# A two-layer hybrid encoder on one core: the groups of the Mamba-2 mixer without modulation tiles, a buffer of its own for the fourth decay piece, and three steps moved between engines

## The chip, the cores and the metric

One NeuronCore of a Trainium2 chip runs the whole program. The metric is the device time of one execution in microseconds; the kernel before took 2819.65 us (median of three).

## The reference, cut to what matters

```python
# SEQ 256, D 2048, two layers, everything float32
cond = silu(c)
shift, scale, gate = split(cond @ ada_w[i, s] + ada_b[i, s], 3)      # i layer, s sublayer: 4 x 6144 columns
h = rms_norm(x, norm_g[i, s]) * (1 + scale) + shift
# layer 0: short convolution mixer, then MLP; layer 1: Mamba-2 mixer, then MLP; x = x + gate * out each time
mlp = square(relu(h @ w1)) @ w2                                       # 2048 -> 8192 -> 2048
# the mixer: 64 heads of 64 in 8 groups, state 128, two chunks of 128 tokens, both directions
z, xbc, dt_raw = split(h @ w_in); xs, B, C = split(silu(conv3(xbc)))
dt = softplus(dt_raw + dt_bias); cum = cumsum(dt * a_neg)             # per direction
y = sum over directions of (C B^T * decay(cum)) @ (dt * xs), plus d_skip * xs
u = group_rms_norm(y * silu(z)) * norm_g; out = u @ w_out
```

## The kernel before, in words

**Units.** Every large product is cut into units: 128 output rows from 2048 input rows and 256 tokens. A unit's weights are two halves of 512 KB, streamed by SP into four `raw` buffers. ScalarE rounds a half into `wh` (`hi`, L687), VectorE makes the rest `wl = raw - wh` (`lo`, L1133), and TensorE runs 32 matmuls, 16 of 512 columns (`wh` against both parts of the input) and 16 of 256 (`wl` against the high part) (`unit`, L936 and L939). Then ScalarE copies the 256 first columns out of PSUM (`copy`, L692) and VectorE adds the others. `lo` of unit v + 2 stands in VectorE's program around the sum of unit v, its first half ahead of the sum and its second behind it. There are 433 units: 48 and 16 of the convolution mixer, 128 of the first MLP, 1 for dt, 50 of groups 0 to 4, 16 of the first half of the mixer's output product, 30 of groups 5 to 7, 16 of the second half, 128 of the second MLP.

**Modulation tiles.** `cond @ ada_w` isn't done on TensorE: 192 tiles of 1 MB are loaded into two buffers `adat`, and VectorE multiplies and sums each (`tile`, L1146), one at the end of some units. Pool keeps the result (`keep`, L496). A tile is only needed when its sublayer begins. The last 48 are shift, scale and gate of the second MLP.

**A group and its scan.** A group is ten units, called slots 0 to 9 here: B, C, four of x, four of z. While group g's units run, the scan of group g - 1 is threaded through them, one piece ahead of each slot on each engine. `scan_piece` stands ahead of a slot's unit and `scan_late` behind it. On TensorE: slot 0 scores and transposes of x; slots 2 to 5 the head products of two heads each, 24 short matmuls (L1049), called batches 1 to 4 here; slot 6 eight transposes; slot 9 two short matmuls that sum squares. On VectorE: `segments` (L1382) makes the exponents of a piece, ScalarE's `decays` (L800) exponentiates them, `masked` (L1313, L1315, L1319) makes the matrix of two heads. Batch k needs piece k, and batch 1 also `xd`, x times dt for both directions, which Pool multiplies (L587) from ScalarE's copies of the transposes (L814). In slot 6 VectorE adds the skip term (L1340) and Pool multiplies by z (L592). In slot 9 ScalarE takes the root (L824), VectorE the reciprocal (L1345) and the scaled result (L1349, semaphore `gu`), ScalarE its high part (L834), Pool its low part (L604, semaphore `u_lo`), which the output product waits for. Pieces 1 and 4 share one buffer, `normt`; so the load of piece 4 waits in slot 2 for batch 1.

**Order.** Every engine runs a program written out by hand, in one order (`walk`); no planner moves anything. SP issues all loads in order, and each load waits until its buffer is free. Groups 1 to 4 are a hardware loop of two iterations of two groups. Group 7's scan runs inside the second half of the output product (`late_outs`), 32 slabs of half a unit, with its slots at the slabs of `SLOT_AT`.

In group 0 the dt path runs in the place of the scan: `dt_late(s)` behind unit s on VectorE, and ahead of it on TensorE. TensorE's part in slot 4 waits for the eleventh of VectorE's small steps.

## Time and profile before

| | us |
|---|---|
| median of 3 runs (2816.4 to 2820.9) | 2819.65 |
| the profiled execution | 2821.6 |
| its span | 2819.9 |

The profiled execution lies 1.7 us above its span and 2.0 us above the median. Times in the rows are us from the start of the span. The page gives, for each engine, the busy time; in 40 slices, its share in tenths and the TensorE clock that was granted; and the chain of work that ended last. The timeline gives each instruction with the idle time before it and what ended that. Stretches can be asked for their busy times and their mean clock.

### The profile page before, as it was taken

What the parts mean: (1) busy time and instruction counts of PE and PEld (TensorE: products, weight loads), DVE (VectorE), ACT (ScalarE), POOL (GpSimd) and SP (SyncE); (2) the same over time, 40 slices, a digit from 0 to 9 for tenths busy, and PEclk for the clock granted to TensorE, in tenths of its full rate; (3) what the DMA queues carried; (4) which work ended last, traced back from release to release, by engine and by line L of the source; (5) the groups of instructions that cost most, each with busy time, mean ns of one, the idle gap of its engine ahead of it and who ended that gap; (6) DMA issues with size and microseconds to landing.
All of it is one profiled execution on the core that took longest, in us unless ns stands there. A gap on an engine that the chain in (4) does not pass through costs nothing.

```text
span 2819.9 us, 46272 instructions
## 1 busy us (share of the span) xinstructions
PE 2607.5 (92%) x14940; PEld 2279.0 (81%) x14940; DVE 2163.9 (77%) x2509; ACT 1359.0 (48%) x2038; POOL 1007.8 (36%) x890
## 2 busy tenths in 40 slices
PE   0399999999999999989999999998999999999998
PEld 0288888888888888878888888887878888888887
DVE  6988889986777779977888878888885555555554
ACT  2244444544444444464555545555455444444454
POOL 3522225442333334534554533555531111111123
PEclk9899999999999999999999999999999999999999
DMA  8888889786877779956565576656646555555554
GB/s 330 308 324 317 304 341 352 242 325 217 285 287 277 281 287 333 356 174 206 202 207 199 180 264 223 208 196 208 228 132 200 187 188 191 187 187 190 189 186 142
DMA packets 171668, 679.60 MB, mean 241 GB/s; under 512 B 18672, under 2 KB 35312, under 8 KB 146704
## 3 DMA queue, kind: packets, MB, share of 16 engines
q1 hardware_dynamic: 171488, 677.75, 68.5%
q8 instruction: 78, 1.28, 0.2%
q14 instruction: 54, 0.44, 0.0%
q0 software_dynamic: 48, 0.13, 0.0%
HBM read 675.58 MB, written 2.23 MB: 240 GB/s over the span
## 4 chain that ended last, share of the span: by engine, by line
PE 73%; DVE 11%; issue 5%; POOL 3%; ACT 3%; DMA 1%; DVEq 0%; ACTq 0%; POOLq 0%; SPq 0%
PE psm L936 45%; PE psm L939 22%; DVE wl L1133 3%; PE psy L1049 3%; DVE adat L1146 2%; ACT wh L687 1%; POOL xd L587 1%; DVE normt L1435 1%; PE psm L1094 1%; PE psr L1094 1%; DMA raw<-in_w 1%; POOL x L534 1%; DVE rbc L1345 0%; PE psm L1097 0%; ACT normt L800 0%
## 5 line engine op out<-in xcount | busy, mean ns | idle before, releaser
L1133 DVE TENSOR_TENSOR wl<-raw,wh 128x1024 fp32r<-128x1024 f32 x862 | 1174.6, 1363 | 410.8 <-ACT wh L687 408.4
L936 PE MATMUL psm<-hcat,wh 128*128 128x512 f32 x3984 | 1269.2, 400 | 5.5 <-DVE tt L1163 4.8
L687 ACT ACTIVATE wh<-raw 128x1024 fp32r<-128x1024 f32 x866 | 911.0, 1052 | 207.6 <-PE psm L939 148.0
L939 PEld LDWEIGHTS psm<-hcat,wl 128*128 128x128 f32 x3984 | 755.8, 190 | 179.7
L936 PE MATMUL psm<-hid,wh 128*128 128x512 f32 x2560 | 806.8, 396 | 11.1 <-POOL hid L604 5.4
L939 PE MATMUL psm<-hcat,wl 128*128 128x256 f32 x3984 | 788.9, 280 | 0.0
L936 PEld LDWEIGHTS psm<-hcat,wh 128*128 128x128 f32 x3984 | 614.4, 191 | 7.2 <-DVE wl L1133 5.5
L939 PEld LDWEIGHTS psm<-hid,wl 128*128 128x128 f32 x2560 | 482.2, 188 | 113.9
L939 PE MATMUL psm<-hid,wl 128*128 128x256 f32 x2560 | 504.1, 278 | 0.0
L1146 DVE CUSTOM_DVE_ANT_0 adat<-adat,cond 128x2048 f32<-128x2048 f32 x176 | 430.3, 2445 | 21.2 <-DMA adat<-in_ada 13.8
L936 PEld LDWEIGHTS psm<-hid,wh 128*128 128x128 f32 x2560 | 391.3, 189 | 12.1 <-POOL hid L604 5.6
L534 POOL TENSOR_TENSOR x<-x,tt 128x256 f32 (+1 forms) x154 | 203.2, 1320 | 404.8 <-DVE tt L1210 404.8
L544 POOL TENSOR_TENSOR hid<-tt,hid 128x256 f32 x128 | 145.6, 1138 | 530.7 <-ACT hid L755 530.7
L496 POOL COPY modc<-modt 128x1 f32 (+1 forms) x192 | 156.4, 820 | 214.8 <-DVE modt L1146 214.7
L692 ACT ACTIVATE ta<-psm 128x256 f32<-128x256 f32 x257 | 97.3, 379 | 209.1 <-PE psm L939 203.8
L692 ACT ACTIVATE ta<-psm,mods 128x256 f32<-128x256 f32 x160 | 75.6, 473 | 223.5 <-PE psm L939 222.6
L755 ACT ACTIVATE hid<-tt 128x256 f32 x128 | 53.5, 418 | 243.2 <-DVE tt L1232 243.2
L1210 DVE SCALAR_TENSOR_TENSOR tt<-psm,mods,ta 128x256 f32<-128x256 f32 x160 | 76.7, 479 | 114.3 <-ACT ta L692 114.1
L572 POOL TENSOR_TENSOR th<-th,acc 128x256 f32<-128x256 f32 x48 | 60.2, 1255 | 242.5 <-ACT th L788 242.5
L958 PE MATMUL psm<-hcat,wh 128*128 128x512 f32 x128 | 47.3, 453 | 77.6 <-POOL wl L669 55.5
L1049 PE MATMUL psy<-xd,normt 128*128 128x64 f32 x384 | 62.0, 335 | 43.4 <-POOL xd L587 37.6
L696 ACT ACTIVATE normt<-x 128x256 f32<-128x256 f32 (+1 forms) x80 | 33.3, 418 | 142.5 <-POOL x L534 100.1
(164 smaller groups left out, 1873.8 us busy)
## 6 DMA issues: line engine op xcount, KB each, us to landing
raw<-in_w SPq DMA_DIRECT2D x866, 512.0 KB, 4.0
adat<-in_ada SPq DMA_DIRECT2D x176, 1024.0 KB, 5.3
xs<-in_ada SPq DMA_DIRECT2D x8, 1024.0 KB, 7.0
zs<-in_ada SPq DMA_DIRECT2D x8, 1024.0 KB, 6.6
normt<-running_sums SPq DMA_DIRECT2D x32, 256.0 KB, 4.6
dec<-running_sums SPq DMA_DIRECT2D x32, 256.0 KB, 5.6
x<-in_xT SPq DMA_DIRECT2D x1, 2048.0 KB, 17.0
out<-x SPq DMA_DIRECT2D x4, 512.0 KB, 2.9
```

The lines of the kernel that those rows point to most:

```text
L496: pool.tensor_copy(modc[:, bass.ds(a.v, 1)], modt[:, a % 2:a % 2 + 1]).then_inc(mod_copied, 1)
L534: pool.tensor_tensor(x[:, nn.v, :], x[:, nn.v, :], tt[:, v % 2, :], ALU.add).then_inc(stored, 1)
L544: pool.tensor_tensor(hid[:, jj.v, T:2 * T], tt[:, v % 2, :], hid[:, jj.v, 0:T].bitcast(F32), ALU.subtract).then_inc(stored, 1)
L572: pool.tensor_tensor(t, t, src, ALU.mult).then_inc(silu_mul, 1)
L687: act.activation(wh[:, h % 4, :], raw[:, h % 4, :], ACT.Copy).then_inc(hi_done, 1)
L692: act.activation(ta[:, v % 2, :], psm[v % 2][:, 0:T], ACT.Copy, scale=scale).then_inc(copied, 1)
L936: pe.matmul(bank[:, :], wh[:, h % 4, (k + i) * P:(k + i + 1) * P], src[:, kb + i, :], start=(kb + i == 0), stop=(kb + i == KB - 1), skip_g ...
L939: mm = pe.matmul(bank[:, T:2 * T], wl[:, h % 4, (k + i) * P:(k + i + 1) * P], src[:, kb + i, 0:T], start=False, stop=(kb + i == KB - 1), s ...
L1049: mm = pe.matmul(psy[ch][:, cols], m[:, at:at + P], xd[:, d, sc, cols], start=(i == 0), stop=(i == 2), skip_group_check=True)
L1133: dve.tensor_tensor(wl[:, h % 4, :], raw[:, h % 4, :], wh[:, h % 4, :].bitcast(F32), ALU.subtract).then_inc(lo_done, 1)
L1146: dve.tensor_tensor_reduce(t, t, cond[:, :], 1.0, 0.0, ALU.mult, ALU.add, modt[:, a % 2:a % 2 + 1]).then_inc(ada_done, 1)
L1210: return dve.scalar_tensor_tensor(out=tt[:, v % 2, :], in0=psm[v % 2][:, T:2 * T], scalar=gcol, in1=ta[:, v % 2, :], op0=ALU.mult, op1=ALU ...
```

## The change

- **Piece 4 has a buffer**: `em[4]` is a part of `adat[:, 1]`. SP loads it right behind piece 3 in slot 0, not in slot 2 behind batch 1.
- **No tiles in groups** (24 before: three in each, slots 4, 5, 8). They go to: the up products of quarters 1 and 2 of the first MLP (three of four units, not two; 8 tiles more), the first output product (12 tiles, not 8), the first 16 units of the second MLP (one in every unit; 16 more). `late_outs` has 4 (slabs 15, 18, 25, 28), not 8 (slabs 1, 4, ..., 22).
- **x copied first**: in slot 0 ScalarE copies the transposes of x (L814) ahead of `decays(g, 1)`, not behind.
- **VectorE multiplies by z** in slot 6, not Pool.
- **Slot 9**: VectorE's reciprocal and its four results (L1345, L1349) stand behind the first `lo` of that slot (`scan_mid`), not ahead of it.
- **Group 0**: `dt_late(1)` and `dt_late(2)` stand ahead of their units on VectorE; the steps of slots 6 and 8 move to 7 and 9.
- **Groups 1 to 4 are written out**, no loop. The first two units of the first output product run interleaved (`pair`), block by block. Head products stay where they are.

```diff
-LATE_TILES = {1 + 3 * k: k for k in range(8)}
+LATE_TILES = {15: 0, 18: 1, 25: 2, 28: 3}
-        em.append(em[1])
+        em.append(adat[:, 1, 0:6 * T].rearrange("p (k t) -> p k t", k=4))
...
-                quarter0(q1, q1 * 16 + (a - 16), (0, 2), False)
+                quarter0(q1, q1 * 20 + (a - 20), (0, 1, 2), False)
...
-                return first_unit(g), (4, 5, 8), g * 3 + a
+                return first_unit(g), (), None
+            for k in range(GA):
+                group(At(k), *g_unit(At(k)))
...
-            bodies(4, lambda i, f: gated(i * 4 + U_OUT0, 2, i * 4, (0, 2), i * 2 + ao, f, False, "chunk 0"))
+                gated(At(U_OUT0 + 4 * k), 2, At(4 * k), (1, 2, 3), At(a + 3 * k), k == 0, False, "chunk 0")
...
-            bodies(4, lambda i, f: relu(i * 4 + U_MLP1, i * 4, i * 4 + 64, 3, (), None, f))
+            bodies(3, lambda i, f: relu(i * 4 + U_MLP1, i * 4, i * 4 + 64, 3, range(4), i * 4 + a, f))
+            relu(At(U_MLP1 + 12), At(12), At(12 + 64), 3, range(4), At(a + 12), False)
...
             def scan_loads(g, s):
-                for piece in {0: (3,), 2: (4,)}.get(s, ()):
-                    load_sums(g, piece)
+                if s == 0:
+                    load_sums(g, 3)
+                    load_sums(g, 4)
...
-                if s == 6:
-                    pool.tensor_tensor(flat(xs, 0, XB), flat(xs, 0, XB), flat(zs, 0, XB), ALU.mult)\
...
-                    decays(g, 1)
                     at_least(act, sg_xt, g + 1)
                     for ch in range(2):
                         act.activation(xd[:, 0, ch, :], psy[ch][:, :], ACT.Copy).then_inc(xt_copied, 1)
+                    decays(g, 1)
...
+                both = first and src == "chunk 0"
+                if both:
+                    pair(u, ready, hid)
...
                 lo(v * 2 + 4)
+                if midway:
+                    midway()
                 at_least(dve, copied, v + 1)
...
+                    dve.tensor_tensor(xs[:, par2, :, :], xs[:, par2, :, :], zs[:, par2, :, :], ALU.mult)\
+                        .then_inc(vz_done, 1)
+            def scan_mid(g, s):
                 if s == 9:
                     at_least(dve, grms, g + 2)
                     dve.reciprocal(rbc[:, :], rbc[:, :]).then_inc(grinv, 1)
...
+                    elif s in (1, 2):
+                        dt_late(s)
+                    unit(g, u + s, s, tiles[s], scanning, midway)
```

## Rows read from the trace of the kernel before

**Rows 1.** The page: span, and busy times by engine.

```profile
span 2819.9 us, 46272 instructions
PE 2607.5 (92%) x14940; PEld 2279.0 (81%) x14940; DVE 2163.9 (77%) x2509; ACT 1359.0 (48%) x2038; POOL 1007.8 (36%) x890
```

**Rows 2.** Stretches: us, busy time by engine (instructions), clock, DMA share, GB/s.

```profile
2200.00:2300.00 100.00, 100.00 (x577) 87.25 (x576) 58.83 (x58) 45.38 (x59) 16.55 (x18) 1.00 0.59 189
1045.00:1125.00 80.00, 80.00 (x461) 69.79 (x461) 73.30 (x81) 38.46 (x57) 36.47 (x25) 1.00 0.90 325
410.00:480.00 70.00, 70.00 (x404) 61.12 (x403) 70.00 (x63) 33.63 (x50) 41.53 (x37) 1.00 0.97 364
```

**Rows 3.** Stretches from batch 4 to batch 4 (periods), and the first output product.

```profile
1347.00:1427.70 80.70, 75.06 (x440) 67.07 (x441) 71.39 (x94) 43.52 (x72) 41.85 (x31) 0.92 0.57 196
1427.70:1507.50 79.80, 71.73 (x439) 63.53 (x437) 69.27 (x94) 45.06 (x75) 40.59 (x30) 0.98 0.59 198
1507.50:1592.40 84.90, 78.65 (x439) 70.44 (x440) 70.20 (x94) 42.85 (x72) 40.50 (x31) 0.88 0.55 186
...
1840.70:1920.50 79.80, 73.59 (x440) 65.80 (x439) 69.39 (x94) 43.86 (x73) 41.41 (x30) 0.94 0.59 198
1920.50:2001.80 81.30, 72.12 (x425) 64.39 (x425) 71.39 (x90) 41.06 (x68) 43.92 (x30) 0.90 0.62 207
...
1592.40:1720.80 128.40, 122.96 (x710) 107.56 (x709) 103.75 (x108) 60.71 (x78) 56.09 (x43) 0.99 0.72 261
```

**Rows 4.** Timeline of TensorE: start, us, what; in brackets idle before it, releaser.

```profile
597.44 0.50 PE L936 MATMUL psm<-hid,wh 128*128 128x512 f32 x1 [2.28 <-POOL hid L544]
1262.35 1.12 PE L1001 MATMUL psr<-ident,xd 128*128 128x128 f32 x4 [5.10 <-DVE xd L1271]
1318.22 2.10 PE L1049 MATMUL psy<-xd,normt 128*128 128x64 f32 x14 [3.16 <-POOL xd L587]
1478.69 1.55 PE L1049 MATMUL psy<-xd,normt 128*128 128x64 f32 x12 [1.14 <-POOL xd L587]
1507.53 1.75 PE L1049 MATMUL psy<-xd,normt 128*128 128x64 f32 x7 [3.79 <-DVE normt L1319]
1634.01 1.22 PE L936 MATMUL psm<-hid,wh 128*128 128x512 f32 x2 [5.44 <-POOL hid L604]
1759.68 1.55 PE L1049 MATMUL psy<-xd,normt 128*128 128x64 f32 x12 [1.42 <-DVE normt L1319]
1891.76 1.54 PE L1049 MATMUL psy<-xd,normt 128*128 128x64 f32 x6 [6.21 <-POOL xd L587]
```

**Rows 5.** Stretches behind a wait of TensorE, with the mean granted clock.

```profile
1261.50:1268.30 6.80, 5.95 (x20) 5.18 (x21) 4.24 (x7) 1.57 (x3) 1.59 (x3) 0.50 0.49 166
1319.50:1326.30 6.80, 6.80 (x28) 6.22 (x28) 4.96 (x10) 4.29 (x8) 1.45 (x2) 0.50 0.22 77
1507.20:1517.40 10.20, 9.87 (x38) 9.20 (x39) 6.50 (x8) 2.51 (x5) 3.85 (x4) 0.50 0.57 183
```

**Rows 6.** Timeline of VectorE, slot 9 of group 6 and slot 0 of group 7.

```profile
1869.70 2.82 DVE L1146 CUSTOM_DVE_ANT_0 adat<-adat,cond 128x2048 f32<-128x2048 f32 x1
...
1880.14 3.10 DVE L1382 SCALAR_TENSOR_TENSOR normt<-normt,gap 128x128 f32<-128x128 f32 x4
...
1887.03 2.92 DVE L1133 TENSOR_TENSOR wl<-raw,wh 128x1024 fp32r<-128x1024 f32 x1
```

**Rows 7.** Timeline of Pool, the same stretch.

```profile
1879.90 2.41 POOL L604 TENSOR_TENSOR hid<-xs,hid 128x1024 fp32r<-128x1024 f32 x1
...
1886.03 5.68 POOL L587 TENSOR_TENSOR xd<-xd,dgrp 128x1024 f32<-128x1024 f32 x2 [3.50 <-ACT xd L814]
```

**Rows 8.** Timeline of ScalarE, the same stretch as rows 6.

```profile
1883.28 1.71 ACT L800 ACTIVATE normt<-normt,ngrp 128x256 f32<-128x256 f32 x4 [4.17 <-DVE normt L1382]
```

**Rows 9.** Timeline of VectorE, two units with a tile each in the first MLP.

```profile
1069.31 2.29 DVE L1146 CUSTOM_DVE_ANT_0 adat<-adat,cond 128x2048 f32<-128x2048 f32 x1
...
1075.00 2.28 DVE L1146 CUSTOM_DVE_ANT_0 adat<-adat,cond 128x2048 f32<-128x2048 f32 x1
```

More of the change, by code:

```diff
@@ L243, in build @@
         dt_act, dt_dve, dt_pe = sem("dt_act"), sem("dt_dve"), sem("dt_pe")
-        cum_out, cb_in = sem("cum_out"), [sem(f"cb_in{i}") for i in range(3)]
+        cum_out, cb_in = sem("cum_out"), [sem(f"cb_in{i}") for i in range(4)]
         par_in, grp_in = sem("par_in"), sem("grp_in")
@@ L386, in load_half, with load_ada @@
                 sp.dma_start(raw[:, h % 4, :], w[h.v]).then_inc(raw_in[h % 4], 16)
[L388 to L389 removed]
+            def load_ada(a, resumed=False):
+                if not a.terms and (a.c >= ADA or a.c - ADA_OUT0 in (0, 1) and not resumed
+                                    or a.c - ADA_LATE in (0, 1) and not resumed):
                     return
@@ L465, in norm, with resume @@
                 sp.wait_ge(out_done, 64)
+            def resume(a, g):
+                at_least(sp, y_head, g * HG)
+                for k in range(2):
+                    load_ada(a + k, True)
             walk(sp, lambda u, j, ada_at, a, f: steps(u, 6, ada_at, a),
@@ L945, in norm_ready, with pair @@
                 return lambda kb: at_least(pe, (hlo_even, hlo_odd)[kb % 2], (n * KB + kb) // 2 + 1)
-            def pair(u, ready):
+            def pair(u, ready, src=hcat):
                 at_least(pe, lo_done, u * 2 + 3)
@@ L982, in ready @@
                         at_least(pe, stored, 3 * (kb + 1))
-                for s in range(4):
+                both = first and src == "chunk 0"
+                if both:
+                    pair(u, ready, hid)
+                for s in range(2 if both else 0, 4):
                     unit(u + s, hid, ready if first and s == 0 else None)
@@ L1147, in tile, with step @@
                                          modt[:, a % 2:a % 2 + 1]).then_inc(ada_done, 1)
-            def step(v, add, rest=None, ada=None, scanning=None):
+            def step(v, add, rest=None, ada=None, scanning=None, midway=None):
                 if scanning:
@@ L1421, in late_outs @@
                         lo(At(2 * U_OUT1 + i + 4))
+                    if slot is not None:
+                        scan_mid(last, slot)
                     for e in late_ends(i, False):
```

113 lines of the change are left out of this document (57 added, 56 removed).

## The prediction

> **What bounds the kernel now.** The page first: TensorE is busy 2607.5 of 2819.9 us [rows 1], so the time can only fall where TensorE waits or runs at its lower clock. The stretches show where it doesn't. In the second MLP it is busy 100 of 100 us with 577 matmuls, 32 to a unit: 5.55 us a unit, and neither VectorE (58.8) nor DMA (0.59) is near a limit. With a tile in three units of four VectorE goes to 73.3 of 80 and the number of matmuls per us stays [rows 2]. So tiles are free in the first MLP, and what is left to gain lies in the groups.
>
> There the stretches from batch 4 to batch 4 are read, "periods" from here. Ten units at 5.55 and about 15 us of short matmuls make about 70; the periods are 79.8 to 84.9 [rows 3]. VectorE isn't full in them either (70 of 80). What the reader is to see is an order, not a load. TensorE comes to batch 1 and waits 6.21 us for Pool's `xd` [rows 4]; but two periods tell more. In the second, TensorE was already late, waited only 1.14 for `xd`, kept its clock, and then waited 3.79 for piece 4 from VectorE's `masked` [rows 4]. Batches 1 and 4 lie 28.84 us apart in it, and 28.8 in a period where the wait stood at batch 1 and the clock fell. So two chains run side by side from batch 1: TensorE needs 28.84 less the 3.8 to 4.0 of waiting, 24.9, at full clock, and VectorE with ScalarE needs about 28.8. A wait ahead of batch 1 costs nothing while TensorE has these 4 us in hand; shortening it alone moves it to batch 4.
>
> **The clock** decides where the wait should stand. The granted clock was 0.50 for 10.2 us behind the wait of 3.79 and for 6.8 us behind those of 5.10 and 3.16 [rows 4, 5]; behind those of 1.14, 1.42 and 2.28 TensorE went on at its higher level. When it falls at batch 1, TensorE's loss is hidden by VectorE's chain. When it falls at batch 4, only TensorE's work follows (units 5 to 9 and 0, 1), and it shows: the third period, which begins so, takes 84.9 where its neighbour takes 79.8 [rows 3]. Price: 5.1 us.
>
> **The steps of a period.** T is the start of batch 4. TensorE is at the next batch 1 at 1891.76 - 6.21 - 1840.7 = T + 44.9 [rows 3, 4].
> - The tile in slot 8 goes: 2.82 us ahead of the reciprocal [rows 6]. But the reciprocal now stands behind a `lo`, and that `lo` behind a `hi` that ScalarE issues after the root; so the reciprocal begins about when it did. What is won is the `lo` itself, which stood behind it: 1.2 us. The tiles of slots 4 and 5 lie where VectorE has time: nothing.
> - x copied first: `xd` waited 3.50 us for ScalarE, behind `decays` of 1.71, which waited 4.17 for `segments` [rows 7, 8]. Now Pool can begin right behind its `hid` and a small copy, 4.4 us earlier, with the 1.2 above: ready at T + 45 or so, not T + 51.
> - But VectorE and Pool block each other. `segments`, four steps of 0.3, took 3.10 beside Pool's 2.41; the `lo` at 1887.03 took 2.92 where a free one takes 1.2, and `xd`, 5.68 for two, holds about 1.0 and 1.1 us of VectorE's work: own time about 3.5 [rows 6, 7]. Before, `xd` held up two `lo`s behind piece 1 (about 3.1 us together). Now it starts while `segments` and `masked` of piece 1 run. If both halves of `xd` get in between, piece 1 ends at 46.3 (1887.03 less 1840.7) - 1.2 + 3.5 = T + 48.6; if only what doesn't fit beside ScalarE's `decays` counts (3.5 - 1.7), at T + 47.0. I take 48.6, since Pool and VectorE took turns instruction by instruction in the rows; both ends stay in the range.
> - From piece 1 to batch 4, VectorE's chain: 28.8 + (1891.76 - 1887.03) = 33.5, less the 3.1 that `xd` no longer takes: 30.4. No load of piece 4 is in it: nothing from its own buffer, which costs nothing either.
> - The product by z leaves Pool for VectorE, about 1.2 us like any of 1024 columns from SBUF, in slot 6, where a tile's 2.3 have just gone. Nothing on the path.
> - So the period is 48.6 + 30.4 = 79.0. TensorE waits about 3.7 at batch 1, the clock falls there, and 24.9 + 5.1 = 30.0 fits under 30.4.
>
> The Trainium skill (SBUF — State Buffer, Who interferes with whom) says that the port pair shared by VectorE and GpSimd is an exclusive lock and that a VectorE instruction with two SBUF inputs contends with a GpSimd instruction that reads SBUF. It speaks against moving `xd` forward, since the lock is then held inside the longer chain. Rows 6 and 7 agree, with 2.92 for 1.2.
>
> **The sum**, against the profiled 2821.6 (2819.9 and 1.7 around it):
> - Groups 0 and 1, to the first batch 4. TensorE's wait of 5.10 for the dt path goes, as its steps come before two units; these delay a sum, 0.8 back. The clock fall behind it, 6.8 us at half, goes: 3.4 [rows 4, 5]. The last dt step is now behind unit 9, its copy, sum and `lo`: TensorE waits about 2.7 for it (estimate from a free `lo`, 1.2, and copies of under 0.5), and `xd` is ready by then, so the 3.16 at batch 1 and the fall behind it (3.4) go; a wait at batch 4 of about 2 grows by 1.6. -5.1 + 0.8 - 3.4 + 2.7 - 6.6 + 1.6 = -10.0.
> - Three periods: 245.4 become 237.0: -8.4 [rows 3].
> - First output product, 128.4. The interleaved pair doesn't reach `u_lo`'s blocks before they are there: the 5.44 and the slow matmuls behind go [rows 4]. But the pair waits for the sum of the last unit, which now stands behind the reciprocal and results: about 3.7, and 1.4 behind the pair for its sums. -1.0.
> - Group 5: batch 4 waited 1.42 for VectorE already [rows 4]. The last unit ahead now has a tile, 2.3, and `xd` starts beside it: +2.4.
> - Two periods, 81.0 and 79.8 before (1759.7 to 1920.5): 79.0 each, and the wait of about 3.8 in group 5 lets the clock fall at a batch 4: +2.3.
> - Late slabs, 81.3 to batch 4 [rows 3]: no tiles there, so VectorE isn't the bound but TensorE: 48.6 + 24.9 + 5.1 = 78.6, -2.7. `u_lo`, for which the last slabs wait, comes 1 us sooner, and VectorE has no tile right behind it: -2.1 together.
> - Eight tiles in quarters 1 and 2: nothing [rows 2]. 16 tiles in the second MLP: VectorE, full in such a unit, takes 1075.00 - 1069.31 = 5.69 from tile to tile [rows 9], against 5.55 to 5.57: +2.2. Its cover is gone there: VectorE and DMA (364 GB/s, 0.97 with a tile in each unit [rows 2]) are both full.
> - Loop gone: TensorE's pause at its turn lay under the wait for `xd`: 0.
>
> Sum: -17.3, 2804 on the profile's scale. The median lies 2.0 below the profiled execution: **2802 to 2803**.
>
> **Rivals.**
> (a) The wait moves to batch 4. If piece 1 ends at T + 47.0, TensorE waits some 2 at batch 1, keeps its clock, and waits 4 at batch 4; each period is then 77.4 + 5.1 = 82.5. -10.0 - 3.0 + 4.1 + 2.4 + 4.2 - 6.0 + 2.2 = -6.1: **2813.5**. For it: 1507.53; it takes but 1.6 us of overlap.
> (b) Piece 1 early and the clock falls at batch 1 all the same, as 2 us of waiting stand ahead of light matmuls: periods of 77.4. -27: **2793**. Against it: 1.14 and 2.28 didn't do it.
> (c) Slower: the clock falls at batch 1 for a short time only, as behind 3.16, and then again at batch 4. A period is 79.0 + 5.1 = 84.1, the third one's size; three periods +1.8, output product +4.1, group 5 +2.4, two periods +7.4, late -3.1, MLP +2.2, groups 0 and 1 -10.0: +4.8, **2824**. It decides from a fall at batch 1 that costs TensorE under 2 us.
> (d) The tiles weren't the matter and the locks eat the rest: groups as before, only the dt path wins, the new tiles cost up to 14 (2 MB a unit at 325 GB/s is 6.5 us): **2818**.
>
> **Chances.** Forecast 0.35, (a) 0.27, (b) 0.14, (c) 0.13, (d) 0.11. A measurement can tell about 0.2%, 5.6 us. Below 2814 lie the forecast, (b) and half of (a): faster 0.63; same 0.21; slower 0.16. The range takes in (a) and most of (b) and stops short of (c): 2793 to 2822.
>
> **What would show it.** Right: `xd` of groups 2 to 7 at its end about T + 45, batch 1 at T + 48 to 49 released by `masked` and not by Pool, no wait above 1 us at batches 2 and 3, periods of 79, no wait for the dt step in slot 4, but one of 2 to 3 ahead of group 1. Clock at half behind batch 1. If it is at half behind batch 4 instead, it is (a) or (c); the sum of waits tells which. Units of the second MLP's first 16 at 5.7; if they take 6 or more, the loads bound. The prediction is wrong as a whole if VectorE's chain from piece 1 to 4 isn't 30 us, since all periods hang on it.

## The result, and the profile after

| | before | after |
|---|---|---|
| median of 16 runs each, us | 2820.57 (2816.4 to 2825.82) | 2827.54 (2817.31 to 2836.99) |
| the profiled execution, us | 2821.6 | 2828.4 |
| its span, us | 2819.9 | 2826.6 |

The ratio of the medians is 1.0025, with an interval of 1.0015 to 1.0036: a quarter of a per cent slower, where 2803 was forecast, with a range up to 2822. The page of the changed kernel, answering to [rows 1]:

```profile
span 2826.6 us, 45095 instructions
PE 2620.2 (93%) x14940; PEld 2289.5 (81%) x14940; DVE 2153.2 (76%) x2517; ACT 1357.3 (48%) x2038; POOL 944.7 (33%) x882
```

TensorE ran the same 14940 matmuls and was busy 12.7 us longer. So the loss isn't waiting: the same matmuls took longer, which is time at the lower clock. Cut at the starts of the batches 4, the span moves like this:

| stretch | before | after | difference | forecast |
|---|---|---|---|---|
| start to the first batch 4 | 1347.0 | 1340.8 | -6.2 | -10.0 |
| three periods | 245.3 | 249.4 | +4.1 | -8.4 |
| batch 4 to the end of the first output product's last matmul | 128.2 | 128.1 | -0.1 | -1.0 |
| from there to batch 4 of group 5 | 39.1 | 41.4 | +2.3 | +2.4 |
| two periods | 160.8 | 161.1 | +0.3 | +2.3 |
| to batch 4 in the late slabs | 81.2 | 78.1 | -3.1 | -2.7 |
| late slabs to the second MLP | 101.4 | 101.2 | -0.2 | -2.1 |
| second MLP to the end | 716.8 | 726.5 | +9.7 | +2.2 |
| sum | | | +6.8 | -17.3 |

Two rows carry the miss: the three periods, off by 12.4 (249.4 for 237.0), and the second MLP, by 7.5.

**The periods.** The stretches of the changed kernel that answer to [rows 3] (us, busy time and instructions of TensorE, weight loads, VectorE, ScalarE, Pool, then the granted clock, DMA share, GB/s), in order of time:

```profile
1340.80:1424.80 84.00, 77.93 (x438) 69.61 (x438) 61.35 (x89) 44.07 (x74) 29.01 (x27) 0.90 0.48 151
1424.80:1506.90 82.10, 76.46 (x439) 68.27 (x439) 61.41 (x89) 44.00 (x74) 29.08 (x27) 0.92 0.47 154
1506.90:1590.20 83.30, 77.52 (x438) 69.23 (x438) 61.32 (x89) 43.74 (x74) 28.98 (x27) 0.90 0.47 152
1759.70:1842.00 82.30, 77.95 (x439) 69.64 (x439) 61.44 (x89) 43.51 (x74) 29.09 (x27) 0.90 0.48 154
1842.00:1920.90 78.90, 74.57 (x439) 66.51 (x439) 61.38 (x89) 44.14 (x74) 29.06 (x27) 0.94 0.52 160
```

VectorE has 61 of 82 us to do, where it had 70 of 80. The time goes roughly with the clock column: 78.9 at 0.94, 82.1 at 0.92, and 82.3, 83.3 and 84.0 at 0.90. TensorE's waits, answering to [rows 4]:

```profile
1297.21 2.05 PE L1041 MATMUL psr<-cT,bT 128*128 128x256 f32 x4 [3.10 <-DVE ncS L1295]
1340.85 1.54 PE L1061 MATMUL psy<-xd,adat 128*128 128x64 f32 x6 [2.94 <-DVE adat L1333]
1394.76 4.95 PE L1061 MATMUL psy<-xd,normt 128*128 128x64 f32 x24 [4.22 <-DVE normt L1333]
1424.85 1.44 PE L1061 MATMUL psy<-xd,adat 128*128 128x64 f32 x10 [1.85 <-DVE adat L1333]
1476.78 5.05 PE L1061 MATMUL psy<-xd,normt 128*128 128x64 f32 x24 [3.72 <-DVE normt L1333]
1506.88 0.32 PE L1061 MATMUL psy<-xd,adat 128*128 128x64 f32 x1 [1.88 <-DVE adat L1333]
1560.12 5.35 PE L1061 MATMUL psy<-xd,normt 128*128 128x64 f32 x24 [5.02 <-DVE normt L1333]
1811.86 5.35 PE L1061 MATMUL psy<-xd,normt 128*128 128x64 f32 x24 [3.91 <-DVE normt L1333]
1841.96 1.22 PE L1061 MATMUL psy<-xd,adat 128*128 128x64 f32 x9 [0.42 <-DVE adat L1333]
1890.75 5.36 PE L1061 MATMUL psy<-xd,normt 128*128 128x64 f32 x24 [3.76 <-DVE normt L1333]
1920.85 1.33 PE L1061 MATMUL psy<-xd,adat 128*128 128x64 f32 x10 [0.57 <-DVE adat L1333]
```

As forecast, batch 1 waits for `masked` (L1333) and not for Pool, for 3.7 to 5.0 us. But there are two patterns behind it. Where the clock is half for 10.2 us behind batch 1 (1811.6), TensorE comes to batch 4 only 0.4 us early. Where it is half for 6.8 (1477.1), TensorE comes 1.88 early, and the clock falls a second time, there. The stretches at half clock, answering to [rows 5]:

```profile
1395.20:1402.00 6.80, 6.80 (x30) 6.41 (x30) 4.99 (x11) 3.33 (x7) 1.58 (x2) 0.50 0.50 157
1425.90:1432.70 6.80, 6.80 (x28) 6.22 (x28) 2.90 (x5) 2.10 (x4) 1.46 (x2) 0.50 0.47 154
1811.60:1821.80 10.20, 9.94 (x38) 9.21 (x39) 8.36 (x15) 5.04 (x10) 1.57 (x2) 0.50 0.32 104
2190.50:2197.30 6.80, 6.11 (x19) 5.24 (x20) 2.99 (x6) 2.38 (x3) 2.22 (x3) 0.50 0.44 142
1296.20:1303.00 6.80, 5.79 (x19) 4.97 (x20) 2.12 (x7) 1.53 (x4) 2.86 (x4) 0.50 0.48 143
1340.60:1350.80 10.20, 9.95 (x38) 9.21 (x39) 4.21 (x6) 2.57 (x5) 2.24 (x3) 0.50 0.34 104
```

The first lies behind a batch 1, the second behind the batch 4 that ends the same period. A fall behind batch 4 costs what it takes from TensorE: 82.1 - 78.9 = 3.2 for 6.8 us at half, 84.0 - 78.9 = 5.1 for 10.2 us. The Trainium skill (TensorE: Matmul & The Clock Gate, Terms) puts the penalty at the throttled time times one less the clock's share; by that rule it would be 3.4 and 5.1, and these rows agree.

So the miss of 12.4 us in the three periods has three parts. The first period takes 84.0 because the clock is half for 10.2 us behind the batch 4 of group 1, at which TensorE waited 2.94 us: 5.0 over the 79.0 of the forecast. The second and the third have a second fall, behind a wait of 1.85 and 1.88, at their start: 3.1 each. In the third, batch 1 also came 1.3 us later than in the second (T + 53.2, not T + 51.9). There ScalarE's rounding of weights ahead of the reciprocal, at 1540.86, stood 1.20 us waiting for its load.

**Piece 1 in the one period of the five that went as forecast** (T = 1841.96), VectorE, then Pool, then ScalarE, answering to [rows 6 to 8]:

```profile
1880.28 6.47 DVE L1403 SCALAR_TENSOR_TENSOR normt<-normt,gap 128x128 f32<-128x128 f32 x4
...
1889.38 1.22 DVE L1333 TENSOR_TENSOR normt<-normt,gcat 128x1024 f32<-128x1024 f32 x1
```

```profile
1880.03 2.41 POOL L613 TENSOR_TENSOR hid<-xs,hid 128x1024 fp32r<-128x1024 f32 x1
...
1882.62 3.98 POOL L601 TENSOR_TENSOR xd<-xd,dgrp 128x1024 f32<-128x1024 f32 x2
```

```profile
1886.78 1.70 ACT L809 ACTIVATE normt<-normt,ngrp 128x256 f32<-128x256 f32 x4 [6.58 <-DVE normt L1403]
```

`xd` ends at 1886.60, T + 44.6; `masked` of piece 1 at 1890.60, T + 48.6; batch 4 starts at 1920.85, 30.1 behind batch 1. Forecast were T + 45, T + 48.6 and 30.4. The order was right, and so was the price of the locks: four `segments` steps take 6.47 us beside `hid` and `xd`, where they took 3.10 [rows 6], so 3.4 more for 3.5 forecast.

**The second MLP.** Its first 16 units, with a tile in each, answering to [rows 2]:

```profile
2100.00:2190.00 90.00, 85.08 (x478) 73.55 (x477) 89.14 (x95) 40.78 (x63) 48.78 (x31) 1.00 0.92 345
```

VectorE is busy 89.1 of 90 us and the tiles are 5.68 to 5.69 us apart, as forecast from [rows 9]. The end of the stretch wasn't foreseen: VectorE's last steps, Pool's last `hid`, TensorE's first matmul of the down product:

```profile
2182.60 2.28 DVE L1158 CUSTOM_DVE_ANT_0 adat<-adat,cond 128x2048 f32<-128x2048 f32 x1
...
2188.28 2.28 DVE L1158 CUSTOM_DVE_ANT_0 adat<-adat,cond 128x2048 f32<-128x2048 f32 x1
```

```profile
2188.89 2.25 POOL L558 TENSOR_TENSOR hid<-tt,hid 128x256 fp32r<-128x256 f32 x1 [2.29 <-ACT hid L764]
```

```profile
2191.20 0.79 PE L945 MATMUL psm<-hid,wh 128*128 128x512 f32 x1 [4.53 <-POOL hid L558]
```

TensorE has done its 16 units and waits 4.53 us for the last hidden block, and then runs at half clock for 6.8 us (2190.5, above).

### The profile page after: what moved, and what is told of

Same layout as the page of the kernel before. It is cut to its first block, busy times and chain, and to the rows that moved or that the text cites. A ratio compares the mean times of both kernels' runs of the same rounds, so it can differ in the third digit from the quotient of the medians.

```text
span 2826.6 us, 45095 instructions
## 1 busy us (share of the span) xinstructions
PE 2620.2 (93%) x14940; PEld 2289.5 (81%) x14940; DVE 2153.2 (76%) x2517; ACT 1357.3 (48%) x2038; POOL 944.7 (33%) x882
## 4 chain that ended last, share of the span: by engine, by line
PE 64%; DVE 18%; issue 6%; ACT 4%; DMA 2%; POOL 1%; DVEq 0%; ACTq 0%; SPq 0%; POOLq 0%
PE psm L945 40%; PE psm L948 20%; DVE wl L1145 6%; DVE adat L1158 2%; ACT wh L696 2%; PE psy L1061 1%; DMA raw<-in_w 1%; DVE normt L1403 1%; PE psm L967 1%; DVE dec L1403 1%; PE psm L1106 1%; ACT dec L809 1%; DVE normt L1460 1%; POOL x L548 1%; DVE acc L1312 1%
## 5 line engine op out<-in xcount | busy, mean ns | idle before, releaser
L1145 DVE TENSOR_TENSOR wl<-raw,wh 128x1024 fp32r<-128x1024 f32 x862 | 1135.7, 1318 | 418.9 <-ACT wh L696 416.6
L945 PE MATMUL psm<-hid,wh 128*128 128x512 f32 x2528 | 798.5, 397 | 10.2 <-POOL hid L558 5.7
L558 POOL TENSOR_TENSOR hid<-tt,hid 128x256 f32 (+1 forms) x128 | 176.4, 1378 | 480.4 <-ACT hid L764 480.4
L548 POOL TENSOR_TENSOR x<-x,tt 128x256 f32 (+1 forms) x154 | 195.5, 1269 | 401.2 <-DVE tt L1224 401.2
L510 POOL COPY modc<-modt 128x1 f32 (+1 forms) x192 | 176.4, 924 | 236.5 <-DVE modt L1158 236.4
L764 ACT ACTIVATE hid<-tt 128x256 f32 (+1 forms) x128 | 53.5, 418 | 267.0 <-DVE tt L1246 267.0
L1224 DVE SCALAR_TENSOR_TENSOR tt<-psm,mods,ta 128x256 f32<-128x256 f32 x160 | 76.6, 479 | 109.2 <-ACT ta L701 109.1
L586 POOL TENSOR_TENSOR th<-th,acc 128x256 f32<-128x256 f32 x48 | 37.8, 788 | 301.1 <-ACT th L797 301.1
L1177 DVE TENSOR_TENSOR tt<-ta,psm 128x256 f32<-128x256 f32 x177 | 73.0, 413 | 22.3 <-ACT ta L701 22.3
## 6 DMA issues: line engine op xcount, KB each, us to landing
x<-in_xT SPq DMA_DIRECT2D x1, 2048.0 KB, 17.3
```

What stands on the lines that cost most here:

```text
L510: pool.tensor_copy(modc[:, bass.ds(a.v, 1)], modt[:, a % 2:a % 2 + 1]).then_inc(mod_copied, 1)
L548: pool.tensor_tensor(x[:, nn.v, :], x[:, nn.v, :], tt[:, v % 2, :], ALU.add).then_inc(stored, 1)
L558: pool.tensor_tensor(hid[:, jj.v, T:2 * T], tt[:, v % 2, :], hid[:, jj.v, 0:T].bitcast(F32), ALU.subtract).then_inc(stored, 1)
L945: pe.matmul(bank[:, :], wh[:, h % 4, (k + i) * P:(k + i + 1) * P], src[:, kb + i, :], start=(kb + i == 0), stop=(kb + i == KB - 1), skip_g ...
L1145: dve.tensor_tensor(wl[:, h % 4, :], raw[:, h % 4, :], wh[:, h % 4, :].bitcast(F32), ALU.subtract).then_inc(lo_done, 1)
L1177: return dve.tensor_tensor(tt[:, v % 2, :], ta[:, v % 2, :], psm[v % 2][:, T:2 * T], ALU.add)
```

## The experiments

Theory A: the changed order gives VectorE's chain of 79.0 a period, and what is lost against it is time at half clock behind batch 4: in two periods the clock's second fall, behind a wait that is short but stands ahead of light matmuls. Rivals: VectorE's chain or its locks got longer; the loads; the product by z. For the MLP: a lag that VectorE never makes good, or only the tile in the last unit.

### Fewer tiles in the second MLP

```diff
-                u, n, nd = q * 32 + U_MLP0, len(tiles), 2
+                u, n, nd = q * 32 + U_MLP0, len(tiles), 2 if last else 3
-            bodies(3, lambda i, f: relu(i * 4 + U_MLP1, ..., 3, range(4), i * 4 + a, f))
+            bodies(3, lambda i, f: relu(i * 4 + U_MLP1, ..., 3, (0, 2), i * 2 + a, f))
```

> The changed kernel with 8 modulation tiles, not 16, in the first 16 units of the second MLP (two of four units), and the 8 others in the down products of quarters 1 and 2 of the first MLP (three of four units, not two). Theory (lag): after the norm VectorE and ScalarE run some 4 us behind TensorE; with a tile in each unit they never catch up, so the first down unit waits 4.9 us for the last hidden block and the clock falls. With 8 tiles the lag goes in five units, as before the change: no wait above 1 us there, full clock, about 9 us less than the changed kernel: 2818 to 2819. Rival (rate): the cost is only the cycle of 5.69 against 5.57, 16 times: 2 us less, and a wait of 3 us or more stays. Rival (loads): the moved tiles cost as much in the first MLP: no gain.

2812.27 us, 0.9973 (0.9963 to 0.9983): 15.3 less than the changed kernel, where 9 was expected. The 9 are where they were looked for, the rest lies in the groups, which nobody touched. From the second MLP to the end it took 717.5, where the changed kernel took 726.5 and the kernel before 716.8. TensorE shows no wait at the down product:

```profile
2097.30:2188.60 91.30, 89.88 (x514) 78.34 (x515) 73.48 (x85) 45.29 (x67) 33.34 (x25) 1.00 0.78 265
```

VectorE has 73.5 of 91.3 us to do in the stretch to the second down unit, and the clock stays up. The 9.0 us are the price of 16 tiles in a row, not of tiles in that MLP: 8 of them cost 0.7. The 8 that went to the down products of the first MLP cost nothing that shows: the first batch 4 came at 1340.7, not 1340.8. That is partly luck: TensorE waited 3.10 us ahead of group 1's scan as in the changed kernel, but the clock didn't fall there. In the groups, where nothing was touched, both patterns of batch 1 came again, in other periods (82.1, 78.9, 79.0; 83.3, 82.0). So it isn't the period's place in the program that decides which pattern comes.

### Extra matmuls in front of the waits: too many, then fewer

```diff
+                if s in (2, 5):
+                    for _ in range(FILLN[s]):
+                        pe.matmul(psr[2][:, T:T + P], ident[:, :], ident[:, :], start=True, stop=True,
+                                  skip_group_check=True)
                 if 2 <= s <= 5:
```

First with 24 at each place in every scan:

> The changed kernel with 24 short dummy matmuls (about 2.7 us at full clock) on TensorE ahead of batch 1 and ahead of batch 4 of each scan, where it waits; nothing else. Theory (clock): VectorE's chain sets the period at 48.6 + 30.2 = 78.9, and all above it is TensorE's lower clock behind batch 4. With the clock kept, the periods of 84.0, 82.0, 83.3 and 82.2 become 78.9 each, 16 us in all, less up to 2 us where the dummies come too late: 2810 to 2814. Rival (light matmuls): the clock falls on the short head products whatever stands ahead: periods unchanged, 2827 to 2830. Rival (TensorE late): the dummies only delay it: 5 us a period, 2850.

2837.59 us, 1.0061 (1.0044 to 1.0078), far above the 2810 to 2814 of its theory. The clock held in all five periods, but TensorE no longer waited anywhere ahead of batches 1 and 4, and all five periods took 80.3 to 80.9:

```profile
1425.07 5.52 PE L1053 MATMUL psr<-ident 128*128 128x128 f32 x48
1430.43 2.79 PE L1066 MATMUL psy<-xd,adat 128*128 128x64 f32 x24
```

24 of them (the trace counts each as two) took 5.4 us, 0.22 each, more than this wait had room for, and twice the 2.7 us reckoned for them. What made the whole kernel slower lies outside the periods, where there was still less to fill: the first batch 4 at 1349.5 for 1340.8, output product and group 5 177.3 for 169.5, late slabs 83.5 for 78.1. A run in which the filling itself is the bound can't tell theory A from its rival. So it was repeated with sizes fitted to the waits:

```diff
# against the run before
+FILL_B1 = (0, 14, 14, 14, 0, 14, 14, 24)
+FILL_B4 = (12, 20, 20, 20, 14, 20, 20, 8)
-                    for _ in range(FILLN[s]):
+                    for _ in range((FILL_B1 if s == 2 else FILL_B4)[g.c]):
```

> The changed kernel, with extra 128x128 matmuls on TensorE in front of its waits, fewer than in the run that had 24 everywhere: 14 before batch 1 and 20 before batch 4 of a period (one took 0.22 us there: 3.1 and 4.5 us), none before batch 1 where TensorE doesn't wait (the scans beside group 1 and beside group 5), 12 and 14 before their batch 4, and 24 and 8 in the late slabs. They write a bank that nobody reads; nothing is left out. Theory (what is lost in the groups is the lower clock behind the two waits, nothing else): no stretch at half clock in the groups, batch 1 still at T + 48.6 behind masked, batch 4 another 30.4 later behind masked, so that the periods are 79.0 where they were 84.0, 82.0 and 83.3, and 79.0 and 79.0 where they were 82.2 and 78.9; with 5 us less in the late slabs, where nothing waits at batch 4. Three periods -12, output product and group 5 -1 to -4, two periods -3, late slabs -3 to -5: 2804 to 2808 in all. Rival (VectorE's chain itself got longer by what changed around it, and the clock is a symptom): the periods stay at 82 to 84 though the clock holds, with longer waits, and the time stays at 2822 to 2828.

2814.73 us, 0.9979 (0.9970 to 0.9989): 12.8 less than the changed kernel. The periods:

```profile
1338.60:1418.20 79.60, 78.02 (x507) 70.15 (x508) 61.73 (x89) 44.13 (x74) 29.39 (x27) 1.00 0.50 159
1418.20:1497.30 79.10, 77.92 (x509) 70.05 (x508) 61.43 (x89) 43.82 (x73) 29.12 (x27) 1.00 0.49 160
...
1824.90:1904.50 79.60, 77.96 (x509) 70.07 (x508) 61.42 (x89) 44.06 (x73) 29.12 (x27) 1.00 0.51 159
```

and batch 1 with what is left of its wait (T = 1418.2, so T + 48.6 again):

```profile
1465.74 0.50 PE L1054 MATMUL psr<-ident 128*128 128x128 f32 x3
1466.83 1.86 PE L1067 MATMUL psy<-xd,normt 128*128 128x64 f32 x15 [0.60 <-DVE normt L1339]
```

The clock is 1.00, and the period is near the 79.0 of the forecast: three periods take 237.8, where 237.0 was forecast and 249.4 measured. (From batch 1 to batch 4 it is 30.4, where VectorE's chain takes 30.1: no wait is left there, and the 20 extra matmuls end last.) TensorE does more work and the kernel is faster. VectorE's program is untouched and its chain as long as before, so the periods of 82 to 84 were TensorE's time at the lower clock: that settles theory A for the periods. The expectation was 2804 to 2808, and what is missing has its place. The late slabs took 80.5 instead of 78.1, where 3 to 5 less was expected: 32 extra matmuls are 7 us, more than the wait there. Output product and group 5 gave 0.2, not 1 to 4: the wait of 3.5 in the product stayed, and VectorE ends last at batch 4 of group 5 whether TensorE waits or is filled.

### x copied second, as before

```diff
                     at_least(act, y_head, g * HG + HG)
                     ...
+                    decays(g, 1)
                     at_least(act, sg_xt, g + 1)
                     ...
                         act.activation(xd[:, 0, ch, :], psy[ch][:, :], ACT.Copy).then_inc(xt_copied, 1)
-                    decays(g, 1)
```

> The changed kernel with ScalarE's order in slot 0 as before (piece 1 is exponentiated first, then x is copied). Theory (two chains): x times dt is ready some 5 us later, about T + 49.8, and locks VectorE behind piece 1 again; but piece 1 itself ends at T + 45.1. TensorE waits about 5 us at batch 1 and none at batch 4, whatever the clock does: periods of 78.5 to 80 with no fall behind batch 4, 10 us less than the changed kernel over four periods: 2817 to 2820. Rival (x first helps): the periods grow by 3 us each: 2840. Rival (same): 2828.

2822.18 us, 1.0006 (0.9996 to 1.0015): 5.4 less than the changed kernel, where 10 was expected. Periods and the waits of the second one, at batch 1 and (none) at batch 4:

```profile
1341.10:1425.20 84.10, 78.39 (x438) 70.25 (x439) 61.51 (x89) 43.06 (x72) 31.16 (x27) 0.88 0.47 151
1425.20:1503.90 78.70, 73.83 (x440) 66.08 (x439) 61.02 (x89) 43.92 (x73) 30.66 (x27) 0.93 0.52 161
```

```profile
1475.02 1.33 PE L1061 MATMUL psy<-xd,normt 128*128 128x64 f32 x5 [4.87 <-POOL xd L601]
...
1503.90 1.34 PE L1061 MATMUL psy<-xd,adat 128*128 128x64 f32 x11
```

Batch 1 waits for Pool's `xd` again, 4.9 to 5.7 us, the clock is always half for 10.2 behind it, nothing waits at batch 4, and no period that begins at full clock takes more than 79.2. So what the change does beside x first (no tiles, piece 4's buffer, z, slot 9) brings one to two microseconds a period by itself: 78.7 to 79.2, for 79.8 to 81.0 in the periods before that begin at full clock; these runs don't part the four. The early `xd` brought batch 1 forward by a microsecond more and made the second fall possible. The two periods of 84.1 and 84.6 are those that begin with a wait of 3.6 to 3.7 behind group 1 and group 5.

### Reciprocal and results ahead of `lo` in slot 9

```diff
-                        scanning, midway = (lambda s=s: scan_piece(g - 1, s)), (lambda s=s: scan_mid(g - 1, s))
+                        scanning = lambda s=s: (scan_piece(g - 1, s), scan_mid(g - 1, s))
...
                         scan_piece(last, slot)
+                        scan_mid(last, slot)
```

> The changed kernel with the reciprocal and its four results ahead of the first weight split of slot 9 again, in the groups and in the late slabs. Theory: without the tile of slot 8 the reciprocal then begins with ScalarE's root and not behind a split that waits for a ScalarE rounding after it: results 2.4 us earlier, the split of 1.2 comes back ahead of the sum; piece 1 ends 1.2 us earlier, T + 47.4, and each of six periods and the late slabs lose about 1 us; but TensorE then waits under 3 us at batch 1 and more often loses its clock at batch 4: 2820 to 2828. Rival (the new place is better by 1.2): 2834.

2824.22 us, 1.0010 (0.9999 to 1.0020). Two of its ten executions took 3737 and 6655 us, for a reason that isn't known; the eight others lie between 2822 and 2826. Batch 1 comes earlier, its wait is 2.78, and in all five periods the clock falls there for 6.8 us and again behind 1.85 to 1.92 at batch 4. The periods are 81.1, 81.1, 79.5, 81.1, 81.1. So piece 1 earlier by 1 us shortens the period by that 1 us against the 82.1 with the same two falls, and isn't enough to get rid of either.

### `xd` held back until `segments` of piece 1 is done

```diff
                     at_least(pool, grp_in, g * 2 + 2)
+                    at_least(pool, seg_done, g * 4 + 1)
                     for d in (1, 0):
```

> The changed kernel, but Pool starts xd only when VectorE has done segments of piece 1 (one more wait on Pool, nothing left out). In the changed kernel three of these four steps took 2.0 to 2.3 us instead of 0.34. Theory (locks between VectorE and Pool set piece 1, and a wait that stands at batch 4 costs the clock there): piece 1 is there at T + 46 to 46.5 and not T + 48.6, TensorE waits 1 to 2 us at batch 1 and keeps its clock, waits 5 to 5.5 at batch 4, and the clock is half for 6.8 or 10.2 us behind it; period 46.2 + 30.4 + 5.1 = 81.7, in all five. Against 249.4 and 161.1 that is -4 and +2; 2824 to 2828. Rival 1 (the lock isn't what makes the steps long): they stay at 2 us beside hid, and piece 1 comes at T + 48 or later. Rival 2 (xd is then so late that batch 1 waits for Pool again): batch 1 at T + 48 or later, released by xd.

2831.32 us, 1.0035 (1.0022 to 1.0047), where 2824 to 2828 was expected: no faster than the changed kernel, whose interval (1.0015 to 1.0036) overlaps this one. VectorE and Pool from slot 9 to slot 0 of a group:

```profile
1466.26 3.13 DVE L1404 SCALAR_TENSOR_TENSOR normt<-normt,gap 128x128 f32<-128x128 f32 x4
...
1471.66 2.12 DVE L1330 TENSOR_TENSOR normt<-normt,gcat 128x256 f32<-128x256 f32 x1
1473.82 1.22 DVE L1334 TENSOR_TENSOR normt<-normt,gcat 128x1024 f32<-128x1024 f32 x1
```

```profile
1469.55 3.95 POOL L602 TENSOR_TENSOR xd<-xd,dgrp 128x1024 f32<-128x1024 f32 x2 [0.89 <-DVE normt L1404]
```

`segments` fell from 6.47 to 3.13 us, but the second half of `xd` now holds one step of `masked` for 2.12 instead of 0.42 (L1329 at 1888.93 in the changed kernel). From the first `segments` step to batch 1 it is 8.9 us instead of 10.5. So the lock explains the long steps, moving it wins 1.5 and not the 2.1 to 2.6 expected, and what it wins moves the wait to batch 4:

```profile
1393.06 3.49 PE L1062 MATMUL psy<-xd,normt 128*128 128x64 f32 x24 [2.89 <-DVE normt L1334]
1423.20 1.12 PE L1062 MATMUL psy<-xd,adat 128*128 128x64 f32 x4 [3.50 <-DVE adat L1334]
```

The clock is half for 3.4 us at the one and 10.2 at the other, and the periods are 82.8, 82.1, 79.6, 81.8, 81.8. This is rival (a), made on purpose: 82.5 was worked out for it. Only its clause that the clock holds at a wait of 2 at batch 1 is wrong: it fell behind each of the five, of 2.17 to 2.90.

The Trainium skill (SBUF — State Buffer, Who interferes with whom) says that the port pair shared by VectorE and GpSimd is an exclusive lock, and that issue order decides who blocks. The rows agree with the lock: the same four steps take 6.47 us beside `hid` and `xd`, and 3.13 when `xd` waits.

### Two tiles moved from last units

```diff
-                gated(At(U_OUT0 + 4 * k), 2, At(4 * k), (1, 2, 3), At(a + 3 * k), k == 0, False, "chunk 0")
+                gated(At(U_OUT0 + 4 * k), 2, At(4 * k), (1, 2, 3) if k < 3 else (0, 1, 2), At(a + 3 * k), k == 0, False, "chunk 0")
-LATE_TILES = {15: 0, 18: 1, 25: 2, 28: 3}
+LATE_TILES = {15: 0, 18: 1, 22: 2, 25: 3, 28: 4}
-            relu(At(U_MLP1 + 12), At(12), At(12 + 64), 3, range(4), At(a + 12), False)
+            relu(At(U_MLP1 + 12), At(12), At(12 + 64), 3, range(3), At(a + 12), False)
```

> The changed kernel with two tiles moved: the one of the first output product's last unit into that chunk's first unit (which had none), and the one of the sixteenth unit of the second MLP into the late slabs. Two places, each read from its own stretch. Output product: with no tile just ahead of group 5, piece 1 there comes 2.3 us sooner: from the end of the product to batch 4 38.9 to 39.2 instead of 41.4, a wait at batch 4 of 1.4 instead of 3.74 and no half clock behind it; the first period after it can then be 79 instead of 82.2. Second MLP: if the wait of 4.92 us for the last hidden block came from VectorE's and ScalarE's lag that a tile in every unit keeps up, it stays at 2.5 us or more and the clock still falls: end stretch 726.5 becomes 724 to 725. If it came only from the tile in that last unit, whose 2.3 us stand beside Pool's hid, the wait is near that of the kernel before, and the stretch 718 to 720. In all 2818 to 2824.

(The first tile moves within the product's last chunk of four, from its last unit to its first.) 2821.21 us, 0.9997 (0.9983 to 1.0012). From the end of the output product to batch 4 of group 5 it is 39.2 instead of 41.4, and the waits there and at the second MLP's down product:

```profile
1756.49 2.89 PE L1061 MATMUL psy<-xd,adat 128*128 128x64 f32 x24 [1.50 <-DVE adat L1333]
```

```profile
2186.86 0.80 PE L945 MATMUL psm<-hid,wh 128*128 128x512 f32 x1 [3.02 <-POOL hid L558]
```

The first was the forecast's +2.4, and it is taken back, though the clock still fell there for 3.4 us. The product itself took 132.9 instead of 128.1, with the clock at half for 6.8 us at 1585.2 and at 1622.7; so in this trace both stretches together take 172.1 and not 169.5, and the gain doesn't reach the total. At the second the wait only falls from 4.53 to 3.02, the clock still falls, and the stretch to the end takes 724.8 for 726.5: the lag is the cause, and the last tile makes a third of the wait.

### Two parts undone: z on Pool, dt steps behind their units

```diff
+                if s == 6:
+                    at_least(pool, v_done, g * XB + 2 * XB)
+                    at_least(pool, stored, first_unit(g) + GU)
+                    pool.tensor_tensor(flat(xs, 0, XB), flat(xs, 0, XB), flat(zs, 0, XB), ALU.mult)\
+                        .then_inc(vz_done, 1)
-                    elif s in (1, 2):
-                        dt_late(s)
```

> The changed kernel with two parts undone that lie in different stretches: the product by z is Pool's again (slot 6), and the dt steps 1 and 2 of VectorE stand behind their unit again, in group 0. Theory for z: nothing, 0 within 1 us per period, as VectorE has room in slot 6 and ScalarE's Square comes behind a tanh and a copy of weights either way; rival: Pool's 2 to 2.5 us there block VectorE, piece 4 or the sum of squares comes later, and a period grows by 1 to 2. Theory for dt: TensorE waits 5 us again in group 0, the clock falls behind it, and the first batch 4 comes 4 to 8 us later than at 1340.8; rival: it was other work of the change (the loop opened, the buffer) that won 6.2 there, and the first batch 4 stays at 1341 to 1343. In all 2830 to 2835 by theory, 2828 by the rival of dt and up to 2840 by that of z.

2834.24 us, 1.0033 (1.0019 to 1.0047).

```profile
1263.59 1.11 PE L1018 MATMUL psr<-ident,xd 128*128 128x128 f32 x4 [5.11 <-DVE xd L1290]
```

The wait of 5.1 [rows 4] is back, and the first batch 4 comes at 1346.9 instead of 1340.8: the dt order is the gain of 6.2 in that stretch, apart from 1.2 us that a fall of the clock at 1225.4, ahead of the dt path, adds in this trace. Pool takes 3.38 us for the product by z, but piece 1 comes only 0.7 us later (T + 49.5 at batch 1 behind a period without a second fall, instead of T + 48.8), and the periods are 82.0, 82.1, 82.8, 82.3 and 79.6. In sum 408.8, where the changed kernel has 410.5: where the clock falls moves more than z does. So z on VectorE was worth 0.7 us in the one place where it can be read alone, and the forecast had nothing for it.

### Versions without and with extra matmuls

Without them: x copied second, 8 tiles in the second MLP, the output product's last tile moved.

> The changed kernel without any extra matmuls, made of three single edits: ScalarE's order of slot 0 as before (decays of piece 1 ahead of the copies of x), 8 tiles in the second MLP instead of 16 with 8 more in the first MLP's down products, and the tile moved from the last unit of the first output product to its first. Nothing is left out. Theory (with x copied second the long wait stands at batch 1, where the clock's fall hides the rest, and no wait of 1.9 us is left at batch 4): periods 78.6 to 79.2 but for the one that begins with a wait of 3 to 4 behind group 1 (84); second MLP 717.5; the one behind group 5, 84.6 with x copied second alone, now 79 to 80, since its wait at batch 4 is 1.5. 2822.2 - 9.0 - 2.3 - 5.0 = 2806 (2803 to 2810). Rival (the sizes of these edits overlap, as the clock's state is carried from stretch to stretch): 2811 to 2816, no better than the tiles alone.

2808.69 us, 0.9953 (0.9940 to 0.9966). That is in its range of 2803 to 2810, but one step of the theory failed: the period behind group 5 took 83.1, not 79 to 80, since the clock fell for 6.8 us behind a wait of only 1.25 at batch 4. In the kernel before it held there behind 1.42 [rows 4].

With them: 8 tiles in the second MLP, the output product's last tile moved, `xd` behind `segments`, and 4 and 22 extra matmuls in a period.

> The version meant to beat both: the changed kernel with 8 tiles in the second MLP instead of 16 and 8 more in the first MLP's down products, the tile moved from the last unit of the output product, Pool's xd behind segments of piece 1, and extra 128x128 matmuls in front of the waits: 4 before batch 1 and 22 before batch 4 of a period, none and 12 or 14 beside groups 1 and 5, 14 and 10 in the late slabs. Nothing is left out. Theory: piece 1 at T + 46.2, clock held at both batches, so that the period is VectorE's chain alone, 46.2 + 30.4 = 76.6, or TensorE's own 69.8 and 26 x 0.22 = 75.5, whichever is longer: 76 to 77 in five periods (410.5 became 386), product and group 5 -4, late slabs -5, second MLP -9: 2827.5 - 26 - 4 - 5 - 9 = 2784 to 2792. Rival (the locks only move: xd now holds masked of piece 1 up): periods of 79 and 2795 to 2800.

2802.02 us, 0.9935 (0.9922 to 0.9949), above its 2784 to 2792. Four periods take 78.0 to 78.1, 1.5 over the 76.6 expected. Of these, 0.9 is VectorE's chain, for which batch 1 still waits 1.3 us and comes at T + 47.1, not T + 46.2. The rest is TensorE from batch 1 to batch 4, 30.9 for 30.1 to 30.4 with 22 extra matmuls there and no wait left at batch 4. The other period took 82.7: 4 extra matmuls left a wait of 2.35 at batch 1, and the clock fell for 10.2 us behind it. So the sizes were changed to 7 and 18:

> The version with all edits (tiles of the second MLP, tile of the output product's last unit, Pool's xd behind segments) and extra matmuls in other numbers: 7 instead of 4 before batch 1, 18 instead of 22 before batch 4 of a period; none, and 14 and 10, beside groups 1 and 5; 18 and 4 in the late slabs. In the run with 4 and 22 TensorE didn't wait at batch 4 at all, so the extra matmuls themselves set the period of 78.0, and in one period a wait of 2.35 at batch 1 took the clock down (82.7). Theory: waits of 0.6 and 1 us, the clock holds in all, periods 77.2 to 77.4 (46.9 + 30.3, VectorE's chain); 2802.0 - 5 x 0.7 - 4.7 = 2794 (2791 to 2797). Rival (VectorE's chain stretches with what comes, or the clock falls somewhere else, at a wait of 1 to 1.5): 2800 or more.

2796.00 us, 0.9915 (0.9902 to 0.9928), in its range of 2791 to 2797 and the best here, 24.6 under the kernel before. Its first two periods, and batch 1 in the second:

```profile
1339.10:1416.60 77.50, 76.20 (x489) 68.15 (x489) 59.95 (x89) 44.04 (x74) 29.19 (x27) 1.00 0.51 163
1416.60:1494.40 77.80, 76.13 (x489) 68.08 (x489) 59.88 (x89) 43.99 (x74) 29.11 (x27) 1.00 0.50 163
```

```profile
1461.43 1.73 PE L1055 MATMUL psr<-ident 128*128 128x128 f32 x14
1464.21 2.86 PE L1068 MATMUL psy<-xd,normt 128*128 128x64 f32 x24 [1.06 <-DVE normt L1340]
```

In the three periods in which the clock held (77.4, 77.8 and 77.4), `xd` behind `segments`, which alone won nothing, goes with 1.3 to 1.7 us less than the 79.1 of the run without it. The two others, with 3.4 us at half behind waits of 0.88 and 1.42 at batch 1, take 77.9 and 78.4. An edit's worth depends on where the clock falls.

## Why the prediction was wrong, by its steps

- **Right:** `xd` at T + 45, piece 1 at T + 48.6, 30.4 from there to batch 4 (30.1 measured), 24.9 for TensorE at full clock, and the 79.0 that they make. Right also group 5 (+2.4; +2.3 measured), the late slabs to batch 4 (-2.7; -3.1), the units of the second MLP (5.69). That the buffer of piece 4 costs and gives nothing was tested by no run.
- **The step that failed:** "the clock falls there, and 24.9 + 5.1 = 30.0 fits under 30.4". It took one size for the fall at batch 1. The measured falls there are 10.2 us in three of the five periods, but 6.8 in the first two. With 6.8, TensorE's path is 24.9 + 3.4 = 28.3, it waits 1.9 at batch 4, and the clock falls again, which takes 3.1 us from the next period. Rows for it stood in the text: behind 3.16 the clock was half for 6.8 us and not 10.2 [rows 5].
- **Rival (c)** is this mechanism, with a chance of 0.13. But its condition, a fall that costs TensorE under 2 us, was too narrow, as 3.4 was enough; and its price of 5.1 for the second fall was too high, as it cost 3.1. That its 2824 lies near the 2827.5 measured is partly luck: it had 2.2 for the second MLP, which took 9.7.
- **The row that misled:** 1.14, 1.42 and 2.28 without a fall [rows 4] were read as showing that a wait of about 2 keeps the clock. The 2.28 stands ahead of 512-column matmuls of a dense unit. Waits of 1.85 to 1.94 at batch 4 were followed by a fall all 14 times that they were there, in six kernels, and 0.91, 1.14, 1.25 and 1.50 were once each. In such a place, 1.42 without a fall in one trace was no bound.
- **A fall that no sum had:** the first period pays 5.0 us for the 10.2 at half behind batch 4 of group 1. The forecast let a wait of about 2 there grow by 1.6, booked a fall behind the like wait in group 5, and none here. It is the largest part of the 12.4, and it has nothing to do with the length of the fall at batch 1.
- **Groups 0 and 1**, -6.2 for -10.0: the wait for the dt path went as forecast. The "about 2.7" for the last dt step measured 3.10 and brought a fall of 6.8 us (1296.2) that the sum didn't have. From there to batch 1 it is 15.8 us, where it is 13.0 in the kernel with fewer tiles, in which the clock held behind the same wait: 2.8 of the 3.8.
- **Second MLP**, +9.7 for +2.2: the term was 16 x 0.13 of rate. Missing was the end of the stretch. The next product needs the last hidden block, which comes through copy, sum, tile, and Pool's `hid` locked beside the tile (2.25 us, where this line's mean was 1.14 before); VectorE, full at 5.69 a unit, never gives back the lag it has after the norm. That is a wait of 4.5 and a fall that costs 3.4 at most. "Tiles are free in the first MLP" was right where VectorE has 73 of 80 us to do, and nearly so with every second unit in the second MLP; it did not hold for every unit.
- **Late slabs to the second MLP**, -0.2 for -2.1: the microsecond by which `u_lo` comes sooner is there, as TensorE waits 3.88 for it (at 2037.60) and not 4.88 (at 2041.33). Of it 0.9 is lost again ahead of the norm, where TensorE waits 3.16 for Pool's `ss` (at 2080.18) and not 2.29 (at 2083.11). Why Pool is later there, and where the other microsecond of the forecast is, stays open.
- **6.8 or 10.2 us:** the size of the wait doesn't tell (3.72 and 3.76 here; in the kernel with fewer tiles 3.73 and 3.73). The start of the fall does. It lies 0.34 us behind the start of batch 1 in the one case and 0.62 ahead of it in the other. Over the 95 falls at batches 1 and 4 in the 13 traces there is no exception: 12 that began 2.03 us or more behind the batch's start lasted 3.4, 35 that began 0.16 to 1.85 behind it 6.8, and 41 from 0.14 behind it to 3.04 ahead of it 10.2; the 7 that began earlier still lasted 13.7 or 17.1. What sets the start isn't shown. Ahead of group 1's scan TensorE waits 3.10 us in seven kernels that are the same up to there: in six the clock fell, 0.4 to 1.2 us before the wait ended and for 3.4 or 6.8 us, and in one it didn't. This may be why the changed kernel's 16 runs spread over 20 us (2817 to 2837), while the five of the last version spread over 6.

## What to carry to other kernels

Where TensorE waits twice in a cycle, the first wait and its clock fall can be cover for the second. Before shortening the first, work out the cycle for each length that the fall has in the trace, not only for the one that fits, and book a fall at every place where the sum leaves a wait of about 2 us or more ahead of light matmuls. A stretch that another engine fills to the brim is paid at its end, by the lag of the chain that the next stage needs, so leave slack in the last units. And where a wait can't be removed, work that keeps TensorE busy in it is worth trying, in an amount under the wait.
